# Layer 0 of a two-block kernel: the rotation table by doublings, plain fp32 ab_in chunks, and D times u as a matmul

## The reference

```python
h = modulate(rms_norm(x, g), shift, scale)
u, q, k, v = split(h @ ab_w_in)               # u: 512 features, q, k, v: 512 each
y_ssm = s5_mixer(u, ...)                      # below
y_att = moba_attention(q, k, v, rel_bias)     # 8 heads of 64
x = x + gate * (concat([y_ssm, y_att]) @ ab_w_out)

# s5_mixer: 32 groups of 64 complex states; a complex scan over the tokens
A_bar = exp(dt * A)                           # = mag * (cos + i sin)
state[t] = A_bar * state[t-1] + B_bar u[t]
y = Re(C state) + D * u                       # then gelu and a gated linear unit (glu)
```

## Time and profile before

| what | value |
|---|---|
| time, three runs | 1524.75, 1525.33, 1529.95 us; median 1525.33 us |
| profiled execution | span 1526.8 us from first to last instruction (no other time is given for it) |
| mean granted TensorE clock | 0.979 of full speed |
| PE busy over the span | 94% (1429.8 us) |
| DVE / ACT / POOL busy | 74% / 51% / 3% |

### The profile page before, as it was taken

The page is one execution under the profiler, slowest core; times in us unless marked ns, Lnnn a source line. Parts: engine busy times, 40 slices in busy tenths (PEclk is TensorE's granted clock), DMA queues, the critical chain, the costliest instruction groups (busy, mean ns, idle before and its releaser), DMA issues.

```text
span 1526.8 us, 24920 instructions
## 1 busy us (share of the span) xinstructions
PE 1429.8 (94%) x9483; PEld 1193.0 (78%) x9483; DVE 1128.1 (74%) x1680; ACT 772.9 (51%) x1090; POOL 51.5 (3%) x38
## 2 busy tenths in 40 slices
PE   5498989999999999999999889999999999999998
PEld 1385568899976668999979655799997877799997
DVE  7999746988884457999984476686667858776666
ACT  3322356555563365555554666564546542455554
POOL 2600200000000000000001000000000000000000
PEclk9898999999999999999999999999999999999999
DMA  9332945988869766988734401355545433345551
GB/s 359 134 129 90 347 162 197 354 318 306 313 242 390 303 230 252 353 342 334 287 147 138 125 0 48 115 186 192 192 170 191 162 111 138 111 169 189 185 196 59
DMA packets 58060, 315.65 MB, mean 207 GB/s; under 512 B 7011, under 2 KB 8524, under 8 KB 33856
## 3 DMA queue, kind: packets, MB, share of 16 engines
q1 hardware_dynamic: 53826, 303.30, 53.8%
q10 hardware_dynamic: 4158, 11.30, 2.3%
HBM read 311.85 MB, written 1.15 MB: 205 GB/s over the span
## 4 chain that ended last, share of the span: by engine, by line
PE 75%; DVE 13%; ACT 5%; issue 4%; DMA 2%; ACTq 0%; SPq 0%; DVEq 0%; POOL 0%
PE bank L2232 62%; DVE w_lo L1339 2%; PE bank L2491 2%; ACT w_hi L751 1%; PE bank L2575 1%; PE bank L2106 1%; PE bank L2124 1%; PE bank L2183 1%; DMA arena<-in_mod_later 1%; PE bank L2300 1%; ACT hf L1256 1%; DVE h_lo L1541 1%; DVE hf L1553 1%; ACT hf L793 1%; DVE hf L1993 1%
## 5 line engine op out<-in xcount | busy, mean ns | idle before, releaser
L1339 DVE TENSOR_TENSOR w_lo<-raw,w_hi 128x2048 fp32r<-128x2048 f32 x186 | 426.2, 2292 | 169.6 <-ACT w_hi L751 168.4
L2232 PE MATMUL bank<-h_hi,w_hi 128*128 128x256 f32 x1800 | 517.3, 287 | 11.3 <-DVE h_lo L1541 9.7
L2232 PE MATMUL bank<-h_lo,w_hi 128*128 128x256 f32 x1800 | 510.8, 284 | 0.0
L2232 PE MATMUL bank<-h_hi,w_lo 128*128 128x256 f32 x1800 | 510.7, 284 | 0.0
L751 ACT ACTIVATE w_hi<-raw 128x2048 fp32r<-128x2048 f32 x186 | 355.8, 1915 | 129.8 <-PE bank L2232 114.6
L2232 PEld LDWEIGHTS bank<-h_hi,w_hi 128*128 128x128 f32 x1800 | 347.1, 193 | 21.3 <-DVE h_lo L1541 11.9
L2232 PEld LDWEIGHTS bank<-h_lo,w_hi 128*128 128x128 f32 x1800 | 347.0, 193 | 2.3 <-issue 0.7
L2232 PEld LDWEIGHTS bank<-h_hi,w_lo 128*128 128x128 f32 x1800 | 346.7, 193 | 0.0
L1756 DVE SCALAR_TENSOR_TENSOR arena<-bank,par,arena 128x255 f32<-128x255 f32 (+1 forms) x264 | 109.1, 475 | 111.5 <-ACT arena L988 79.1
L2232 PE MATMUL bank<-w_hi,a_hi 128*128 128x512 f32 x368 | 145.8, 396 | 4.9 <-DVE a_lo L1781 4.0
L2232 PE MATMUL bank<-w_hi,a_lo 128*128 128x512 f32 x368 | 144.3, 392 | 0.0
(11 more groups left out here) (327 smaller groups left out, 1703.5 us busy)
## 6 DMA issues: line engine op xcount, KB each, us to landing
raw<-in_stream SPq DMA_DIRECT2D x186, 1024.0 KB, 5.0
arena<-in_mod_stream SPq DMA_DIRECT2D x64, 768.0 KB, 7.5
arena<-in_mod_later SPq DMA_DIRECT2D x48, 512.0 KB, 8.0
raw<-in_mod_pe SPq DMA_DIRECT2D x36, 512.0 KB, 6.6
arena<-in_mod_pe SPq DMA_DIRECT2D x12, 512.0 KB, 12.7
sq<-row_store ACTq DMA_DIRECT2D x7, 512.0 KB, 3.5
sq<-in_bias SPq DMA_DIRECT2D x8, 256.0 KB, 6.7
x<-in_x_t ACTq DMA_DIRECT2D x1, 1024.0 KB, 8.6
```

The lines of the kernel that those rows point to most:

```text
L1339: nc.vector.tensor_tensor(w_lo[s][:], raw[s][:], w_hi[s][:].bitcast(F32), ALU.subtract).then_inc(lo_done, 1)
L2232: ins = nc.tensor.matmul(out_, l, r, start=first and n == 0, stop=last and n == 2, **kw)
```

## The change

Four edits are made together.

1. **Table by doublings.** `e_pair` and GpSimd's share of it are gone. DVE builds the first 64 columns of all 16 tiles by six doublings. Each tile then doubles twice more, 64 to 128 and 128 to 256. One such step is a `twist(j, m)` on ACT (two scaled copies) and a `double(j, m)` on DVE (one operation). These stand four and two tiles ahead of the scan in the program's order.
2. **Plain chunks.** The eight ab_in chunks are not split. PE multiplies the raw fp32 weights by the fp32 h, 16 matmuls for a chunk instead of 48. `h_hi` and `h_lo` of this norm are gone; ACT writes four of the eight h tiles and DVE the other four. A raw slot is free only when its chunk is done (`chunk_done`), where it was free after `w_hi` and `w_lo`. The lists of `hi` and `lo` now begin at chunk 8, the first of glu.
3. **D·u on PE.** A diagonal matrix `skip_diag` makes D·u one more matmul for four tiles, in front of y_of(0), (4), (8) and (12). `y_out` becomes an ACT copy.
4. **Slots and loads.** Pieces 4 to 7 of eight slots lie in the raw slots. `ssm_b` and `ssm_c` move from ACT's queue, where they went first, to SP's, behind the pieces. Chunk 0 is issued after piece 13 (it was after piece 11), and chunk 1 waits for 14 used pieces.

```diff
@@ SP: loads
-                if q >= SLOTS:
-                    sp.wait_ge(hi_done, q - SLOTS + 1 + more)
-                    sp.wait_ge(lo_done, q - SLOTS + 1 + more)
+                if q >= SLOTS + PLAIN:
+                    sp.wait_ge(hi_done, q - SLOTS + 1 - PLAIN + more)
+                    sp.wait_ge(lo_done, q - SLOTS + 1 - PLAIN + more)
+                elif q >= SLOTS:
+                    sp.wait_ge(chunk_done, q - SLOTS + 1)
...
             for m in range(PM_FIRST):
                 load_pm(m)
-                if m == 11:
+                if m == 13:
                     load_plain("ab_in", 0, 1)
+            sp.dma_start(b_turned, A["ssm_b"].rearrange("p (e t s) -> p e t s", e=2, t=UT)).then_inc(sem("b_landed"), 16)
+            sp.wait_ge(sem("pm_used"), 14)
             load_plain("ab_in", 1, 2)
+            sp.dma_start(c_raw, A["ssm_c"].rearrange("p (e j c) -> p e j c", e=2, j=ST)).then_inc(sem("c_landed"), 16)
@@ ACT
+            def twist(j, m):
...
+                k = m // BASE - 1
+                nc.scalar.activation(turns_[:, j, 0, m:2 * m], turns_[:, j, 1, 0:m], ACT.Copy, scale=pow_neg[:, k, j:j + 1])
+                nc.scalar.activation(turns_[:, j, 1, m:2 * m], turns_[:, j, 0, 0:m], ACT.Copy, scale=pows[6 + k][:, 1, j:j + 1])\
+                    .then_inc(sem("twisted"), 1)
...
                 nc.scalar.activation(dst, src, ACT.Copy).then_inc(bank_free, 1)
                 hi_upto(q + 3)
+                twist(c + 4, BASE)
+                twist(c + 2, 2 * BASE)
+                if c == 6:
+                    y_out(0)
...
             for h in range(HEADS):
+                if h < 4:
+                    twist(12 + h, BASE)
+                if h < 6:
+                    twist(10 + h, 2 * BASE)
+                if h == 0:
+                    y_out(1)
+                if h == 5:
+                    y_out(2)
                 if h:
                     probs(h - 1)
...
                 if h:
                     head_copy(h - 1)
+            y_out(3)
@@ DVE
+            x_scaled(0)
+            for k in range(6):
+                m = 1 << k
+                lo_, up = turns_[:, :, :, 0:m], turns_[:, :, :, m:2 * m]
...
+            def double(j, m):
+                k = m // BASE - 1
+                dve.wait_ge(sem("twisted"), doubling(j, m))
+                nc.vector.scalar_tensor_tensor(turns_[:, j, :, m:2 * m], turns_[:, j, :, 0:m], pows[6 + k][:, 0, j:j + 1],
+                                               turns_[:, j, :, m:2 * m], ALU.mult, ALU.add).then_inc(sem("doubled"), 1)
...
             for c in range(8):
                 lo_upto(Q["ab_in"] + c + 3)
+                double(c + 4, BASE)
                 ssm_tile(c)
-                if c in (2, 4):
-                    link(e_pair(nc.vector, link, 1 + c // 2))
-                if c == 6:
-                    y_out(0)
+                double(c + 2, 2 * BASE)
             for h in range(HEADS):
-                if h % 2 == 0:
-                    dve.wait_ge(sem("e_ready"), h // 2 + 1)
+                if h < 4:
+                    double(12 + h, BASE)
                 ssm_tile(8 + h)
-                if h == 0:
-                    y_out(1)
-                if h == 5:
-                    y_out(2)
+                if h < 6:
+                    double(10 + h, 2 * BASE)
@@ PE
+                    nc.tensor.matmul(half(Y_BANK[n], 0), skip_diag[:, n, :], u_t[:, n, :], start=True, stop=False, skip_group_check=True)
...
+            def plain_chunk(c, q, fill):
+
+                w = raw[q % SLOTS]
...
+                    if AB[c] < 6:
+                        sides = w[:, part], hf[:, k, :]
+                    else:
+                        sides = hf[:, k, n * P:(n + 1) * P], w[:, k * 256:k * 256 + 256]
+                    ins = nc.tensor.matmul(half(4 + fill % 2, n), *sides, start=c > 0 and k == 0, stop=k == DT - 1, skip_group_check=c == 0)
+                ins.then_inc(chunk_done, 1)
```

More of the change, by code:

```diff
@@ L75 @@
 CM_GROUPS = (2, 0, 3, 1)
+PLAIN = 8
 def consts():
@@ L488, in build, with doubling @@
         Y_BANK = (2, 6, 2, 5)
[L489 to L502, removed]
+        DOUBLED = [(j, BASE) for j in range(4)] + [(j, 2 * BASE) for j in range(2)]
+        for _c in range(8):
+            DOUBLED += [(_c + 4, BASE), (_c + 2, 2 * BASE)]
+        for _h in range(6):
+            DOUBLED += [(_h + 12, BASE)] * (_h < 4) + [(_h + 10, 2 * BASE)]
+        def doubling(j, m):
+            return DOUBLED.index((j, m)) + 1
         FILL, _f = {}, 0
@@ L885, in _, with y_out @@
                 x_square(0, j, BY_TOKENS)
-            pm_copy(0)
+            def twist(j, m):
+                i = doubling(j, m)
+                if i == 1:
+                    act.wait_ge(sem("doubled"), 1)
+                if m == 2 * BASE:
+                    act.wait_ge(sem("doubled"), 1 + doubling(j, BASE))
+                k = m // BASE - 1
+                nc.scalar.activation(turns_[:, j, 0, m:2 * m], turns_[:, j, 1, 0:m], ACT.Copy, scale=pow_neg[:, k, j:j + 1])
+                nc.scalar.activation(turns_[:, j, 1, m:2 * m], turns_[:, j, 0, 0:m], ACT.Copy, scale=pows[6 + k][:, 1, j:j + 1])\
+                    .then_inc(sem("twisted"), 1)
+            pm_copy(0)
+            for j in range(4):
+                twist(j, BASE)
+            pm_copy(1)
+            act.wait_ge(sem("gates_known"), 1)
+            for k in (0, 1, 4, 5):
+                if k % 4 == 0:
+                    act.wait_ge(sem("x_turned"), 3 + k // 4)
+                nc.scalar.activation(hf[:, k, :], turned(0, k), ACT.Identity, scale=gains[:, 0, k:k + 1], bias=mod[:, 0, k:k + 1])\
+                    .then_inc(sem("full_ready"), 1)
+            for j in range(2):
+                twist(j, 2 * BASE)
             act.wait_ge(sem("both_sum"), 1)
             nc.scalar.activation(both_q, both_q, ACT.Sqrt).then_inc(sem("both_q_ready"), 1)
[L889 to L892, removed]
+            def y_out(n):
+                act.wait_ge(sem("ssm_y_done"), 4 * n + 4)
+                nc.scalar.activation(u_t[:, n, :], half(Y_BANK[n], 0), ACT.Copy).then_inc(sem("y_ready"), 1)
             for c in range(8):
@@ L1425, in _ @@
[L1425 to L1429, removed]
-            crb, cib = (v.unsqueeze(2).broadcast_to([P, ST, 32]) for v in (cr, ci))
-            c_of = [c_turned[:, e].rearrange("p a (b c) -> p (a b) c", c=32) for e in range(3)]
@@ L1605, in _ @@
+            def double(j, m):
[3 more added lines that the diff above has]
+                                               turns_[:, j, :, m:2 * m], ALU.mult, ALU.add).then_inc(sem("doubled"), 1)
+            for j in range(4):
+                double(j, BASE)
             first_mod_out(0, 2)
             x_gains(0)
-            x_lower(0)
@@ L1608, in _ @@
-            lo_upto(2)
-            link(e_pair(nc.vector, link, 1))
+            for k in (2, 3, 6, 7):
+                if k % 4 == 2:
+                    dve.wait_ge(sem("x_turned"), 3 + k // 4)
+                nc.vector.tensor_scalar(hf[:, k, :], turned(0, k), gains[:, 0, k:k + 1], mod[:, 0, k:k + 1], ALU.mult, ALU.add)\
+                    .then_inc(sem("h_ready"), 1)
+            for j in range(2):
+                double(j, 2 * BASE)
+            dve.wait_ge(sem("c_landed"), 16)
+            crb, cib = (v.unsqueeze(2).broadcast_to([P, ST, 32]) for v in (cr, ci))
```

208 lines of the change are left out of this document (102 added, 106 removed).

## The result

The changed kernel is slower by half a per cent: median 1536.96 us of 20 runs (1529.98 to 1544.95), against 1529.91 us of 20 runs of the kernel before (1524.75 to 1532.75). The ratio is 1.005, with a 95% interval of 1.0036 to 1.0065. The three runs of before that stood ahead of the prediction lay at the low end of what 20 runs then showed, so the change is sized by the two medians of 20 runs, 7.0 us apart, and not against 1525.33.

What follows compares the result with a forecast made beforehand. PE was taken as the bound over the whole, with transfers, then DVE, then PE setting the pace in the first 128 us. Heads -0.5, tail +0.46 and +0.97 gave +0.9 us: 1526 us, range 1515 to 1534.

Steps and rivals of the forecast that it cites:

- The start: Up to chunk 0: last piece near 31.6, chunk 0 begins at 34.9 and ends at 42.1 us, a gain of 22.7.
- The chunks: Eight plain ab_in chunks on PE: 7.16 us each for 5.94, period 10.06, chunk 7 ends at 111.5, 16.4 earlier.
- the four passes of the Trainium skill: Rival for the ab_in chunks on PE: four passes against the split's three, 7.92 us a chunk, 1532 us, chance 0.05.
- Behind chunk 7: Load and split ahead of tile 7: 8.0 us after the chunk's end for 4.6, tile 8 at 125.1, 12.2 gained.
- The heads: Head rounds: head_turn(0) at 138.6, 10.5 us gained; by head_turn(3) at 173.4 only 0.5 gained.
- the ring: Head rounds: head_turn, pieces, head_out, head_copy, twist, double, tile, double, recip, probs wait in a circle, 10.95 us warm, 6.98 before.
- the cold round: Head round with PE at the lower clock: head_turn 1.12, pieces 4.50, 13.6 us in all.
- the middle between warm and cold: Heads: head_turn(3) put at 173.4 us, between 171.2 warm and 175.5 cold; 0.5 gained.
- The tail: Behind the heads: one more skip_diag, 0.46 us, and Gelu 0.97 later behind y_out(3) and the table load.
- The rival without a ring: Heads: tiles of rounds 1 to 3 don't wait for head_copy, 1516 us; chance 0.25, shared with a partly hidden ring.
- a dearer chunk: Rival for ab_in on PE: from 8.0 us a chunk, 6.7 us more, slower by over 0.5%; chance 0.07.
- a late start: Rival at the start: DVE's doublings take twice the estimate, DVE ends 7.2 us late, 1533 us; chance 0.05.

Runs made afterwards that it cites:

- the experiment: Changed kernel with the split of the first glu and ab_out chunks moved behind the scan tile on DVE and behind the twists on ACT: 1529.98 us, ratio 0.9999.
- the second run with extra matmuls: Changed kernel with small extra matmuls on PE where it waits, written into the other half of bank 5: 1534.33 us, ratio 1.0045.
- the kernel before with the wait: Kernel before with only a wait added: DVE holds tiles 10 and 11, and the step behind 12 and 13, for an earlier head_copy: 1536.89 us, ratio 1.0055.

## Why the prediction was wrong

**The start: right.** The last piece landed at 31.5 (31.6 forecast, 34.3 before), and chunk 0 began at 34.66 (34.9). It took 8.86 us instead of 7.2, since the clock stood at 0.72 from 34 to 40; of the profiles of seven other kernels with the same start, five have the copy behind it at 41.5 to 42.4 (42.1 forecast) and two at 43.3 and 43.5.

**The chunks: right.** They take 7.17 (7.16 forecast), a period 10.0, and the copy behind chunk 7 came at 113.31 (111.5), 1.8 late, of which 1.5 come from chunk 0. By the four passes of the Trainium skill ("FP8 and Floating Point Precision", section TensorE Precision Notes) the estimate was 7.92; the trace does not agree and keeps to the row. What I did not ask is what a plain chunk is worth: with GpSimd's table left out the split start is only 6 us later, and seven further chunks cost an estimated 8.5 us on PE (1.22 each).

**Behind chunk 7: the load was mis-sized.** It landed 4.7 us after the chunk (3.8 forecast), so w_hi began at 118.01, tile 7 at 122.43 (119.7) and tile 8 at 127.84 (125.1). From the copy to tile 7 it is 9.1 us, 4.5 more than the 4.6 of before, where the forecast added 3.6 with a doubling. The 7 us of the experiment are another size: with the split behind the tile, the 4.6 that before also paid ahead of tile 7 go too.

**The heads: the ring was right in every link, and its length was the term that failed.** The forecast had 10.95 us warm (full clock), 13.6 cold (lower clock), and 34.8 us from head_turn(0) to head_turn(3); the profile has 13.4, 16.7 and 9.5, 39.6 together. It also began 4.6 late: 1.8 from the chunks, 0.9 from the load, and the rest from two long doublings ahead of probs(0). The first round was as long as forecast (13.5, cold), but by luck: its head_turn and pieces ran partly at the full clock (0.66 and 3.87 us, where the cold ring has 1.12 and 4.50), and its doubling behind the tile was 0.8 longer. The second round was given 12 to 14 and took 16.7, 3.1 beyond even the cold 13.6, because three links were short. The pieces take 6.1 us, from 157.57 to 163.68, and not 4.5 (1.6 more): the cold round was made without the pm_turn in the middle of the pieces, which the trace of before has in this round too (at 161.29). From head_out to head_copy it is 1.7, and not 1.0 (0.7 more): that link was left at its warm length. And the doubling of 256 columns beside GpSimd's part of the tile takes 1.36 to 1.37 us, not 0.45, once ahead of head(0) and once in each of the first rounds (0.8 more until recip starts). Even near the full clock, in the second run with extra matmuls, this round takes 13.1, 2.2 over the warm one. I then took the middle between warm and cold, where PE waits nearly 5 us in each of the first rounds and the clock fell in each: cold was the likelier end.

**The tail: right.** Gelu began at 213.17, 30.4 us after head_turn(3), where it was 28.6 before: 1.8 us longer, 1.43 forecast. It stands 0.01 us behind the table load (1.28 from 211.88):

```profile
211.47 0.38 ACT L906 ACTIVATE arena<-bank 128x256 f32<-128x256 f32 x1 [0.60 <-PE bank L2335]
211.88 1.28 ACT L973 ACT_TABLE_LOAD   x1
213.17 0.72 ACT L973 ACTIVATE arena<-arena 128x256 f32<-128x256 f32 x2
```

**The sum.** 0.9 us were forecast and 7 came. In the profiled execution the end is 16.3 us later than in the trace of before. 4.6 of them are the late begin of the heads, 4.8 the ring, 0.3 the tail and 0.9 what was forecast; the other 5.7 come behind Gelu, which is 10.6 late. The forecast said that nothing changes there. But the same work, from 730 us on before and from 742.8 on after, took 3.4 us longer, at a lower granted clock (0.95 for 0.97):

```profile
730.00:985.00 255.00, 236.76 (x1410) 187.08 (x1409) 167.35 (x302) 150.89 (x271) 5.25 (x2) 0.97 0.35 124
```
```profile
742.80:1001.20 258.40, 240.82 (x1406) 191.43 (x1409) 167.35 (x302) 150.71 (x271) 5.25 (x2) 0.95 0.35 122
```

Against the trace of before, the five versions with the ring lose 1.7 to 5.7 us between Gelu and the end, and the five without it gain 1.0 to 3.5, in one profile each. Why is open, and so is how the 7 us of the median divide between the heads and what follows. The top of the range, 1534, gave 2.1 us for cold rounds; in the profile the second and third round took 4.9 more than the middle that was forecast.

The rival without a ring (1516) is the version with the doublings moved out, 10.7 us under before; the changed kernel itself showed nothing of it. The rivals of a dearer chunk and of a late start are out: 7.17 us per chunk, and DVE's part was done ahead of pm_turn. One row was read too strongly, without effect on the sum: the 1.08 us in the earlier trace rows are the wait of the weight load, and PE itself was idle for 0.20 there.

## What to carry to other kernels

A small operation that one engine prepares for another belongs where both are idle: put into a loop whose engines already pass work round, it closes a ring, and the ring's whole length is paid in each turn. When several edits are made together, look at them one by one: here leaving GpSimd's table out of the start gave 20 us, and the whole change, which builds that table in another way, lost 7 until the doublings and the late split were moved. For a step that waits and then works, take the lower clock as the case, not the middle, where the trace already shows it at that place.

## What the runs showed of the hardware

GpSimd's fp32 multiplies stretched DVE's operations in the start by 1.3 to 2.7 times: w_lo 3.02 for 2.29 us, two h_lo 2.56 for 0.94. A doubling of 256 columns took 1.36 to 1.37 us where GpSimd worked on the sine part, and 0.48 elsewhere. Not every operation is stretched: y_out, also of 256 columns but with one input in PSUM, took 0.48 us at 141.42 while GpSimd worked in the trace of before:

```profile
140.79 1.72 POOL L733 TENSOR_TENSOR arena<-arena 128x512 f32<-128x512 f32 x1 [78.02 <-DVE arena L1621]
```

Which property of the operation decides is not shown.

The other half of bank 2 was taken for unused when the extra matmuls were put there. By the Trainium skill ("PSUM — Partial Sum Buffer", section The four PSUM rules) a matmul that starts a sum clears the written marks of its whole bank, in the groups of 32 partitions that it writes (here all 128), so that the next matmul into a running sum there overwrites it. That it is D times u of tiles 9 to 11 that goes is argued from this and from PE's order, where extra matmuls stand right behind y_of(8); no run here looked at the sums themselves.

The changed kernel's 20 runs spread over 15 us; those of the kernel before (14 to 20 runs a chip) over 7 to 11, those of the versions without the ring (4 to 7 runs) over 3 to 11, and those of the kernel before with the wait (7 runs) over 7. The slowest three of its 20 runs had granted clocks of 0.968 to 0.973, the fastest two 0.981.
